# The last head of a gated DeltaNet layer: two output-weight rows split earlier on ScalarE and GpSimd, a gate's SiLU and the scaled keys later, one low part moved from GpSimd to VectorE

## The reference, cut to what matters

```python
qkv, z, b_raw, a_raw = jnp.split(x @ w_in, ...)        # 8 heads of 128, times q, k, v, z
qkv = jax.nn.silu(causal_depthwise_conv(qkv, conv_w))
q, k = l2_normalize(q), l2_normalize(k)
beta, g = sigmoid(b_raw), -exp(a_log) * softplus(a_raw + dt_bias)
o = gated_delta_rule(q, k, v, beta, g)                 # chunks; a triangular inverse per chunk
o = rms_norm(o, norm_g) * jax.nn.silu(z)
y = o.reshape(B, S, 1024) @ w_out                      # sums over the heads
```

## Time and profile before

| what | value |
|---|---|
| median of 3 runs | 1774.6 us (1773.81 to 1775.4) |
| the profiled execution | 1774.9 us |
| its span | 1773.2 us |
| mean granted PE clock | 0.985 |
| PE, PEld busy | 96%, 73% of the span |
| DVE, ACT, POOL busy | 50%, 44%, 18% of the span |

### The profile page before, as it was taken

One profiled execution on the slowest core, in us unless ns is written; L12 is line 12 of the kernel. 1 busy time (PEld: TensorE's weight loads), 2 busy tenths in 40 slices (PEclk: granted clock), 3 DMA queues, 4 the chain that ended last, 5 costly groups with the idle time before them and its releaser, 6 DMA issues. The chain is left out here.

```text
span 1773.2 us, 28853 instructions
## 1 busy us (share of the span) xinstructions
PE 1697.7 (96%) x11189; PEld 1294.3 (73%) x11189; DVE 881.4 (50%) x1655; ACT 788.4 (44%) x1288; POOL 313.2 (18%) x243
## 2 busy tenths in 40 slices
PE   9899999999999899799989999999999999899898
PEld 6777777777777677678777887666666666687786
DVE  5647566575766635844331200344444454577433
ACT  4646456464554722142222311556555565531411
POOL 5213212122222241300000000222221221012000
PEclk9999999999999999989989999999999999999899
DMA  6111011210101121041130201111111101041411
GB/s 157 49 37 38 24 49 18 56 37 25 49 13 56 43 99 68 25 153 45 39 109 16 80 2 43 41 45 32 45 40 37 45 21 40 19 161 40 138 45 51
DMA packets 113528, 94.43 MB, mean 53 GB/s; under 512 B 19761, under 2 KB 95729, under 8 KB 113393
## 3 DMA queue, kind: packets, MB, share of 16 engines
q1 hardware_dynamic: 113392, 92.59, 18.2%
HBM read 84.08 MB, written 8.49 MB: 52 GB/s over the span
## 5 line engine op out<-in xcount | busy, mean ns | idle before, releaser
L435 PE MATMUL gdn_unit<-part_hi,gdn_w_hi 128*128 128x512 f32 x496 | 226.3, 456 | 0.0
L437 PE MATMUL gdn_unit<-part_hi,gdn_w_lo 128*128 128x512 f32 x496 | 195.5, 394 | 0.0
L436 PE MATMUL gdn_unit<-part_lo,gdn_w_hi 128*128 128x512 f32 x496 | 194.4, 392 | 0.0
L2106 DVE CUSTOM_DVE_ANT_0 fa_probs<-fa_scores,fa_decay 128x896 f32<-128x896 f32 (+7 forms) x128 | 97.1, 758 | 121.0 <-PE fa_scores L1918 73.6
L867 DVE SCALAR_TENSOR_TENSOR x<-gdn_raw,gdn_taps,x 128x512 f32<-128x512 f32 x144 | 130.3, 905 | 30.6 <-ACT x L665 25.8
L399 POOL TENSOR_TENSOR gdn_w_lo<-ring,gdn_w_hi 128x1024 fp32r<-128x1024 f32 x31 | 75.6, 2437 | 238.5 <-ACT gdn_w_hi L645 238.5
L2052 ACT ACTIVATE fa_probs_t<-fa_turned 128x512 f32<-128x512 f32 (+1 forms) x96 | 52.3, 545 | 139.0 <-PE fa_turned L1935 138.4
L2046 ACT ACTIVATE fa_probs<-fa_probs,fa_top 128x896 f32<-128x896 f32 (+7 forms) x128 | 99.4, 777 | 22.1 <-DVE fa_top L2106 18.4
L437 PEld LDWEIGHTS gdn_unit<-part_hi,gdn_w_lo 128*128 128x128 f32 x496 | 93.3, 188 | 21.0
L1295 PE MATMUL e_gate<-e_w_hi,part_hi 128*128 128x512 f32 x256 | 103.1, 403 | 2.9 <-DVE part_lo L1432 2.8
L435 PEld LDWEIGHTS gdn_unit<-part_hi,gdn_w_hi 128*128 128x128 f32 x496 | 94.0, 190 | 16.1 <-issue 3.9
(11 more groups left out here) (327 smaller groups left out, 3697.6 us busy)
## 6 DMA issues: line engine op xcount, KB each, us to landing
ring<-in_gdn_w_in_dram SPq DMA_DIRECT2D x31, 512.0 KB, 4.1
ring<-in_ple_w_gate_dram SPq DMA_DIRECT2D x32, 256.0 KB, 3.1
ring<-in_fox_w_in_dram SPq DMA_DIRECT2D x32, 256.0 KB, 3.1
ring<-in_fox_w_in_dram SPq DMA_DIRECT2D x16, 512.0 KB, 4.8
fa_decay<-c_rows_scratch SPq DMA_DIRECT2D x64, 128.0 KB, 3.1
gdn_g_bc<-g_rows_scratch SPq DMA_DIRECT2D x8, 512.0 KB, 8.7
x_scratch<-x SPq DMA_DIRECT2D x8, 512.0 KB, 2.9
m_old<-x_scratch SPq DMA_DIRECT2D x8, 512.0 KB, 3.5
```

What stands on the lines that cost most here:

```text
L435: pe.matmul(out, w_hi[:, j % 2, k, :], xh[:, k, ts], start=(k == 0), stop=False)
L436: pe.matmul(out, w_hi[:, j % 2, k, :], xl[:, k, ts], start=False, stop=False)
L437: mm = pe.matmul(out, w_lo[:, j % 2, k, :], xh[:, k, ts], start=False, stop=(k == KT - 1))
L2106: step(dve.tensor_tensor_reduce(probs[:, n % 3, blocks(e)], scores[head][:, blocks(e)], decay[:, head, blocks(e)], 1.0, 3e38, ALU.add, ALU ...
```

## The change

It has four parts, all in the last head of `delta_net`. In the diff below the first function is the one on POOL, the next places are on ACT, and the last is on DVE.

1. `OUT_ROWS` becomes (0, 0, 10, 14, 16, 18, 20, 22). ACT makes the high parts of rows 0 and 1 right behind the copy of the last projected unit, ahead of v's SiLU; POOL makes their low parts at step 0, ahead of q's decay at step 2. The rows 3 to 7 stand two steps earlier than before.
2. SiLU of z moves from the end of `it == 7` to step 40 of `it == 8`.
3. The scaled keys move on ACT from step 3 to step 13, behind the scaled values, for the last head alone.
4. The low part of the first o tile moves from POOL, step 10, to DVE, step 11.

```diff
-OUT_ROWS = tuple(range(10, 26, 2))
+OUT_ROWS = (0, 0, 10, 14, 16, 18, 20, 22)
+AT_FIRST_O_PART = 11
+AT_LATE_SILU = 40
...
             def out_work(s):
-                if s in O_PARTS:
+                if s in O_PARTS[1:]:
                     t = O_PARTS.index(s)
                     pool.wait_ge(o_high, t + 1)
+                    pool.wait_ge(o_low, t)
                     step(pool.tensor_tensor(w_lo[:, t % 2, 0:H - 1], o_t[:, 0:H - 1, t * P:(t + 1) * P],
                                             w_hi[:, t % 2, 0:H - 1].bitcast(F32), ALU.subtract), o_low)
-                if s in OUT_ROWS:
-                    k = OUT_ROWS.index(s)
+                for k in (k for k in range(KT) if OUT_ROWS[k] == s):
                     pool.wait_ge(out_high, k + 1)
...
-                if s in OUT_ROWS:
-                    k = OUT_ROWS.index(s)
+                for k in (k for k in range(2, KT) if OUT_ROWS[k] == s):
                     act.wait_ge(out_loaded[k % 3], 16 * (k // 3 + 1))
...
-                    if s == AT_KEYS:
+                    if s == (AT_KEYS if it < H else AT_VALUES + 1):
                         act.wait_ge(k_turned, p + 1)
...
-                if it < H:
+                    if it == H and s == AT_LATE_SILU:
+                        z = qkvz[:, (H - 1) % 2, 3]
+                        step(act.activation(z, z, ACT.Silu), z_ready)
+                if it == H - 1:
+                    take_unit(it, 7)
+                    for k in range(2):
+                        act.wait_ge(out_loaded[k], 16)
+                        step(act.activation(xh[:, k], out_raw(k), ACT.Copy), out_high)
+                    v = qkvz[:, it % 2, 2]
+                    act.wait_ge(conv_made, 6 * it + 6)
+                    step(act.activation(v, v, ACT.Silu), v_ready)
+                elif it < H:
...
+                    if it == H and s == AT_FIRST_O_PART:
+                        dve.wait_ge(o_high, 1)
+                        step(dve.tensor_tensor(w_lo[:, 0, 0:H - 1], o_t[:, 0:H - 1, 0:P],
+                                               w_hi[:, 0, 0:H - 1].bitcast(F32), ALU.subtract), o_low)
```

## The result

The changed kernel takes 1777.97 us (median of 20 runs, 1776.6 to 1780.2) against 1774.76 for the kernel before in the same comparison (20 runs): ratio 1.0018, 95% interval 1.0012 to 1.0024. The forecast was 1777.7. The time lies 0.3 us above it and inside the range, and 0.18% is on the slow side of what was called no measurable change; with 20 runs of each kernel the interval excludes "no difference".

What follows compares the result with a forecast made beforehand. PE bounds the kernel, in the last head by its 4.42 us wait for POOL's low part. 2.05 us (first piece) plus 1.1 (second wait) give +3.1, forecast 1777.7 us (+0.17%), own range 1776.5 to 1779.0, with rivals 1772.4 to 1779.8.

Steps and rivals of the forecast that it cites:

- `inv` 4.95 us later by three turns on POOL: Last head: three POOL operations each hold one of DVE's eight `inv` operations in turn, so `inv` comes 4.95 us later.
- Rival A: DVE's `inv` operations keep their turn (1772.8 us) or, second form, are not held at all (1771.8 us); chance 14%.
- The first piece 2.05 later: PE's first piece in the last head starts at 621.6 instead of 619.56, with the transpositions ahead at 1.2 GHz.
- The half clock costs what it did before: PE runs some 3.3 us at half speed behind the first piece, as before; at the bounds 0.8 us less.
- B's condition: Rival B, the half clock stays: past 627 it decides, costing 0.5 us per further us, to 1779.0 or 1779.7; chance 18%.
- A second wait that adds 1.1: PE's third-level product waits for ACT's copy behind row 6 and its DMA, at 635.1 instead of 634.0: 1.1 us more.
- the second wait hides most of that: Said of the 0.8 us gained if the half clock ends earlier: the wait behind row 6 hides most of it.
- The sum, +3.1: First piece 2.05 us later plus 1.1 for the second wait: 3.1 us for the whole kernel.
- PE runs full as before: Behind the third level no later wait is longer, so PE runs as before and the 3.1 us stays.

Runs made afterwards that it cites:

- e2: The changed kernel with POOL waiting until DVE has made `inv` before taking the low parts of rows 0 and 1: 1774.03 us, ratio 0.9995.
- e3: The changed kernel with row 1's low part computed twice on POOL, so four operations instead of three meet DVE's `inv` operations: 1780.48 us, ratio 1.0035.
- e1: The changed kernel with the scaled keys back at step 3 on ACT, where ACT waits for the transposed `inv`: 1777.11 us, ratio 1.0009.
- e5: The changed kernel with 42 instead of 20 dummy products of PE before the transposition of `inv`: 1778.51 us, ratio 1.0016.
- e11: The changed kernel with 42 dummy products and rows 5, 6 and 7 behind the copies they stood in front of: 1776.32 us, ratio 1.0007.
- e4: The kernel before with only the first o tile's low part moved from POOL to DVE: 1777.1 us, ratio 1.0010.
- e10: The kernel before with only the first o tile's low part on DVE, e4 run a second time: 1777.1 us, ratio 1.0008.
- e7: e4 with ten more dummy products of PE behind the values' transposition: 1773.61 us, ratio 0.9991 to the kernel before.
- e8: The kernel before with fourteen more dummy products of PE in its wait for the first o tile's low part: 1773.5 us, ratio 0.9986.
- e9: e6 with row 5 behind the second level's copy, row 6 behind the third's and row 7 behind the fourth's: 1770.17 us, ratio 0.9970.
- e6: The changed kernel with rows 0 and 1 split on DVE, not POOL; q's decay behind row 7, keys behind row 3: 1774.47 us, ratio 0.9994.

## Why the prediction was right, step by step

- **`inv` 4.95 us later by three turns on POOL.** Shown: 4.93 from the entry (12.09 against 7.16). The pattern was the drawn one, two free operations, three held, three free. The forecast had the held ones end 2.50 us apart; they end 2.49 and 2.48 apart. e2 takes the turns away and the loss with them, e3 adds one and the loss grows by 2.0 us at `inv`. Rival A, in both its forms, is gone; so is what the page "Advanced Engine Details and Errata" of the Trainium skill, section "VectorE Performance Modes", would let one expect, that such operations run free. What the Trainium skill says in "SBUF — State Buffer", section "Who interferes with whom", fits these traces: 2.45 to 2.47 us for an operation of 0.42, beside operations of 2.40 on POOL.
- **The first piece 2.05 later.** Shown: 2.03, released by DVE's low part (1.09 us, forecast 1.1), after transpositions at half clock (1.11 and 1.94 us, where the earlier trace rows have 0.66 and 1.06).
- **The half clock costs what it did before.** Only nearly. The windows have it from 0.66 in 614 to 616 to 0.78 in 624 to 626, against 0.86 in 618 to 620 and 0.58 in 622 to 623 before; its tail behind the first piece made the first level 0.33 us later than the first piece's own 2.03. B's condition, a clock of 0.50 past 627, did not come about.
- **A second wait that adds 1.1.** As drawn: the third level's product came at 634.95 on before's scale (forecast 635.1), released by the copy behind row 6, 3.03 us later than before. So 1.00 was added to 2.03. PE waited 0.59 of it; most of the rest it had already lost to the clock's tail, which without row 6 would have been the loss in its place. e1 and e5 show why the split is hard to see: take away either the half clock or the rows in front of the copies, and the other one is there with nearly the same due time. The forecast had this for the clock alone ("the second wait hides most of that"). What it missed is how nearly they cover each other; e11, which takes both away, brings the sixth level back to before's place with `inv` still 5 us late.
- **The sum, +3.1.** In the trace +3.03 at the third level and, unchanged, at the sixth; in the time +3.2 between the two medians. The upper end of the forecast's own range, 1779.0, is 0.3 above what its terms give (1777.7 + 0.8 + 0.2).
- **"PE runs full as before" behind it.** Held for the waits: after the third level its next wait is the one of 1.85 us for DVE that it had before too, ahead of 645.11 there and of 647.41 here. It did not hold for the clock. With 0.60 instead of 1.00 in 648 to 652 the kernel after takes 43.59 us from the sixth level to the last product of the pieces, where the kernel before takes 42.02, so that product is 4.60 late. That the profiled execution ends only 3.03 late, counted from the entry (spans of 1775.5 and 1773.2 us), is because the 1.57 came back behind the pieces, where in these two executions it was the kernel before that had more of the half clock. The forecast had both at nothing; that they cancel to the hundredth is luck.

What was not foreseen: part 4 of the change, the o tile on DVE, which the forecast took for a gain of its own, costs 1.9 us when done alone (e4, e10). Dummies of PE take that away (e7), but how the loss comes about is not shown.

## What to carry to other kernels

Before filling an engine's idle time with POOL work, look at what DVE does in those microseconds: if it reads two SBUF operands, each POOL operation can hold one DVE operation for its whole length; here that cost some 2 us each time, on an operation of 0.42 us as on one of 1.09. An engine in order should do what is due first: a split of a row that is due six steps later, standing in front of a copy that is due now, passes its DMA's wait to PE. When a removed wait brings nothing, look for two covers of the same width before concluding that it was not the bound, and look at the clock behind every wait: here dummies of PE in an existing wait were worth 1.9 us of the time by themselves (e8). And before explaining a difference of a few us by one profile, see where in the span it arises.

## What the runs showed of the hardware

- DVE and POOL really alternate: in the kernel after and in e3 each POOL operation of 2.40 us let through exactly one DVE operation of 0.42, which took 2.45 to 2.47 us with its wait. It goes both ways: in e2 DVE's held operation made POOL's next one 3.10 us. DVE operations with an operand in PSUM were not held: the one at 612.37 in e2 took its 0.69 us while POOL worked from 611.75 to 616.55.
- The granted clock fell to 0.50 in or behind waits of PE as different as 1.41 us (e9), 3.36 (e2, e4) and 5.56 (the kernel after), and stayed at 1.00 in e7 beside waits of 1.13 and 1.65, and in e6 at the same wait of 1.41, in the same order, behind which it fell in e9. It also fell in places where the order had not changed: the window 640 to 650, with PE busy for 8.15 us in each of them, has 1.00 in the kernel before (below), 0.94 in the kernel after and 0.83 in e11. What decides it there was not found. From the sixth level to the last product of the pieces nine of the fourteen profiled executions take 42.0 to 42.1 us; the five in which the clock fell there (after, e3, e6, e10, e11) take 43.4 to 43.6. From that product to the end of the span, where all fourteen kernels have the same instructions, they take 1087.0 (after) to 1090.7 us (e10). So a single profile can't settle a difference of some 3 us in the time: in e10 the sixth level comes 0.6 earlier than in the kernel before, and the time is 2.1 longer.

```profile
640.00:650.00 10.00, 8.15 (x70) 6.29 (x68) 3.96 (x10) 2.81 (x4) 2.10 (x1) 1.00 0.40 127
```

The granted clock is the third number from the end.
